# The up projection as one 512-column matmul per weight block, with both halves' sums ahead of a weight split, and that split on VectorE alone

## The reference, cut to what matters

```python
D_MODEL = 2048; SEQ = 256; GRID_W = 64; D_FF = 5632

def conv_glu_ffn(h, w_up, conv_w, w_down, grid):
    up = h @ w_up                          # (256, 2048) @ (2048, 11264)
    up = dwconv2d_grid(up, conv_w) if grid else dwconv1d(up, conv_w[1])
    a, b = jnp.split(up, 2, axis=-1)
    return (jax.nn.silu(a) * b) @ w_down   # (256, 5632) @ (5632, 2048)
```

## Time and profile before

| | before |
|---|---|
| median of three executions | 2902.12 us |
| profiled execution, its own time | 2901.94 us |
| its span | 2899.9 us |
| TensorE busy | 2783.1 us (96%) |
| VectorE busy | 1893.0 us (65%) |
| ScalarE busy | 996.5 us (34%) |
| GpSimd busy | 567.7 us (20%) |
| stretch of the 22 passes of the up projection | 2111.8 to 2626.9 us |
| in it from 2143.1: TensorE / VectorE busy | 483.8 / 433.1 of 483.8 us |

### The profile page before, as it was taken

One profiled execution on the slowest core, in us unless ns is written; L12 is line 12 of the kernel. 1 busy time (PEld: TensorE's weight loads), 2 busy tenths in 40 slices (PEclk: granted clock), 3 DMA queues, 4 the chain that ended last, 5 costly groups with the idle time before them and its releaser, 6 DMA issues.

```text
span 2899.9 us, 66324 instructions
## 1 busy us (share of the span) xinstructions
PE 2783.1 (96%) x25890; PEld 2094.7 (72%) x25890; DVE 1893.0 (65%) x3509; ACT 996.5 (34%) x1684; POOL 567.7 (20%) x708
## 2 busy tenths in 40 slices
PE   5899999999999999999988999999899999999997
PEld 1346666656666665666655888887789999998886
DVE  1136776666777666777675656564588999896444
ACT  1133333233333223333221433333344444443332
POOL 0012322223321222331220200000023333330000
PEclk8899999999999999999999999999999999999999
DMA  8721233321223322223234545554535555554554
GB/s 329 325 81 57 89 103 110 104 97 57 88 96 110 110 96 65 83 88 110 81 105 157 191 163 193 181 188 168 187 123 182 186 178 186 177 184 160 185 183 138
DMA packets 75801, 412.84 MB, mean 142 GB/s; under 512 B 9296, under 2 KB 11984, under 8 KB 42608
## 3 DMA queue, kind: packets, MB, share of 16 engines
q1 hardware_dynamic: 74864, 408.10, 40.5%
q0 software_dynamic: 768, 2.10, 0.2%
HBM read 405.38 MB, written 4.19 MB: 141 GB/s over the span
## 4 chain that ended last, share of the span: by engine, by line
PE 90%; DVE 4%; DMA 2%; ACT 2%; issue 1%; SPq 0%; DVEq 0%; ACTq 0%; PEldq 0%
PE PB L714 21%; PE Q L977 12%; PE Q L972 6%; PE PB L972 4%; PE PB L967 4%; PE CH L972 3%; PE PB L968 3%; PE CH L967 3%; PE CH L968 3%; PE Q L850 3%; PE Q L836 3%; DMA ring<-w_mod_dram 2%; PE Q L857 2%; PE CH L891 2%; PE CH L873 2%; PE CH L901 1%
## 5 line engine op out<-in xcount | busy, mean ns | idle before, releaser
L714 PE MATMUL PB<-hT,ring 128*128 128x512 f32 (+1 forms) x1536 | 670.7, 551 | 1.0
L1703 DVE TENSOR_TENSOR w_lo_r<-ring,w_hi_r 128x1536 fp32r<-128x1536 f32 (+3 forms) x178 | 389.9, 2190 | 204.4 <-ACT w_hi_r L1290 204.4
L1290 ACT ACTIVATE w_hi_r<-ring 128x2048 fp32r<-128x2048 f32 (+2 forms) x178 | 325.8, 1830 | 314.2 <-PE PB L972 104.0
L714 PEld LDWEIGHTS PB<-hT,ring 128*128 128x128 f32 x1536 | 256.1, 189 | 114.3 <-issue 69.8
L968 PE MATMUL PB<-hT_r,w_hi_r 128*128 128x256 f32 x832 | 204.7, 286 | 0.0
L1989 POOL TENSOR_TENSOR w_lo_r<-ring,w_hi_r 128x512 fp32r<-128x512 f32 x88 | 118.1, 1342 | 356.9 <-ACT w_hi_r L1290 356.9
L1878 DVE TENSOR_TENSOR w_lo_r<-ring,w_hi_r 128x1408 fp32r<-128x1408 f32 x62 | 100.7, 1626 | 131.9 <-ACT w_hi_r L1409 131.9
L1558 DVE SCALAR_TENSOR_TENSOR arena<-ring,csilp,arena 128x512 f32<-128x512 f32 x240 | 180.5, 752 | 6.1 <-DMA ring<-w_mod_dram 1.5
L967 PE MATMUL PB<-hT_r,w_hi_r 128*128 128x256 f32 x704 | 175.9, 289 | 2.8 <-DVE hT_r L1805 2.8
L977 PE MATMUL Q<-ff_r,w_hi_r 128*128 128x512 f32 x704 | 174.4, 395 | 3.5 <-ACT w_hi_r L1409 3.5
L967 PE MATMUL CH<-hT_r,w_hi_r 128*128 128x256 f32 x704 | 170.9, 283 | 0.0
(11 more groups left out here) (268 smaller groups left out, 5335.8 us busy)
## 6 DMA issues: line engine op xcount, KB each, us to landing
ring<-w_up_dram SPq DMA_DIRECT2D x88, 1024.0 KB, 4.8
ring<-w_mod_dram SPq DMA_DIRECT2D x128, 512.0 KB, 3.6
ring<-w_rkv_dram SPq DMA_DIRECT2D x48, 1024.0 KB, 6.0
ring<-w_down_dram SPq DMA_DIRECT2D x64, 704.0 KB, 4.0
ring<-w_mod_dram SPq DMA_DIRECT2D x32, 1024.0 KB, 9.3
ring<-w_ga_dram SPq DMA_DIRECT2D x16, 1024.0 KB, 4.8
ring<-w_gb_dram SPq DMA_DIRECT2D x16, 1024.0 KB, 4.9
ring<-w_pa_dram SPq DMA_DIRECT2D x16, 1024.0 KB, 4.9
```

The source lines that it names most:

```text
L714: last = mm(PB[slot % 2][:, 0:cols], tile(n, kt), hT[:, kt, 0:cols], start=(kt == 0), stop=(kt == KT - 1))
L1290: f(w_hi_r[:, r % 2, 0:n], ring[:, r, 0:n], ACT.Copy).then_inc(hi_rdy, 1)
L1703: tt(w_lo_r[:, r, 0:n], ring[:, r, 0:n], as_f32(w_hi_r[:, r % 2, 0:n]), ALU.subtract).then_inc(lo_rdy, 1)
```

## The change

Of each up tile, the first two products are now one matmul of 512 columns: 16 of them write the whole bank (`hT_r[:, kt]` holds low activations in columns 0 to 255 and high ones in 256 to 511), and the 16 of the low weight are added to the upper half of the bank. The two halves then have to be added. ScalarE copies the lower half to SBUF (`us[r]`, 256 columns, new), VectorE adds the upper half from PSUM to it (`add_halves`, new), and from then on the centre tap and all other taps read `us[r]` in SBUF. The adds of tiles 0 and 1 stand ahead of `low` of tile 2, and those of tiles 2 and 3 ahead of `low` of the next tile 0. The bank is free again after its add (`up_sum`), not after the taps. In the diff come TensorE's part, ScalarE's, VectorE's four and GpSimd's, in this order. `low` covers all 2048 columns, and GpSimd's part of it is gone; GpSimd keeps `ff_split`.

```diff
-POOL_COLS = 4 * P
+        us = [woven_sb[:, r].rearrange("p c t -> p (c t)")[:, 0:T] for r in range(4)]
...
             def up_four(i, first):
                 for r in range(4):
                     high_ready("up", i, r)
-                    pe.wait_ge(up_cv, i * 2 + 1 + r // 2)
+                    pe.wait_ge(up_sum, i * 4 + r + 1)
                     for kt in range(KT):
                         if first and r == 0:
                             pe.wait_ge(h_rdy, KT + kt + 1)
-                        with_high(four[r][:, 0:T], r, kt, h2_hi_r[:, kt], h2_lo_r[:, kt], kt == 0)
+                        mm(four[r][:, :], w_hi_r[:, r % 2, kt * P:(kt + 1) * P], hT_r[:, kt], start=(kt == 0), stop=False)
                     low_ready("up", i, r)
-                    pe.wait_ge(up_lo, i * 4 + r + 1)
                     for kt in range(KT):
-                        last = with_low(four[r][:, 0:T], r, kt, h2_hi_r[:, kt], kt == KT - 1)
+                        last = with_low(four[r][:, T:TT], r, kt, h2_hi_r[:, kt], kt == KT - 1)
...
                     if r % 2 == 0:
+                        act.wait_ge(up_cv, i * 2 + r // 2 + 1)
+                    f(us[r], four[r][:, 0:T], ACT.Copy).then_inc(up_half, 1)
+                    if r % 2:
                         act.wait_ge(ff_rdy, i * 2 + r // 2 + 1)
-                    f(cv[r], four[r][:, 0:T], ACT.Identity, scale=convw_a[:, r, 4:5]).then_inc(up_mid, 1)
+                        for q in (r - 1, r):
+                            act.wait_ge(up_sum, i * 4 + q + 5)
+                            f(cv[q], us[q], ACT.Identity, scale=convw_a[:, q, 4:5]).then_inc(up_mid, 1)
...
-                r, n = r % 4, width(phase, r % 4) - (POOL_COLS if phase == "up" else 0)
+                r, n = r % 4, width(phase, r % 4)
...
-                        last = stt(grid(cv[r])[:, orow, ocol], grid(four[r][:, 0:T])[:, irow, icol],
+                        last = stt(grid(cv[r])[:, orow, ocol], grid(us[r])[:, irow, icol],
...
+            def add_halves(i, r):
+
+                dve.wait_ge(up_half, i * 4 + r + 1)
+                tt(us[r], us[r], four[r][:, T:TT], ALU.add).then_inc(up_sum, 1)
...
                     taps(i - 1, 1, 1, carry)
+                add_halves(i, 0)
+                add_halves(i, 1)
                 lows("up", i, 0, FT // 2, "down")
...
                 taps(i, 0, 1, prev)
+                add_halves(i, 2)
+                add_halves(i, 3)
                 lows("up", i, 2, FT // 2, "down")
...
-                    pool.wait_ge(hi_rdy, split_count("up", i, r))
-                    pool.sem_inc(seen, 1)
-                    nc.gpsimd.tensor_tensor(w_lo_r[:, r, REG - POOL_COLS:], ring[:, r, REG - POOL_COLS:],
-                                            as_f32(w_hi_r[:, r % 2, REG - POOL_COLS:]), ALU.subtract).then_inc(up_lo, 1)
```

More of the change, by code:

```diff
@@ L337, in layer_kernel @@
         pool_lo = sem("activation_low_ready")
-        up_lo = sem("up_weight_low_ready")
         h2_raw = sem("h2_ready")
@@ L354, in layer_kernel @@
         xr_ld = sem("x_reloaded")
+        up_half = sem("up_low_activation_half_copied")
+        up_sum = sem("up_halves_added")
         up_mid = sem("up_centre_tap_done")
@@ L1068, in _ @@
             pe.sem_inc(up_cv, 2)
+            pe.sem_inc(up_sum, 4)
             pe.sem_inc(ff_rdy, 2)
@@ L1813, in taps @@
             def taps(i, j, half, prev):
-                if half == 0:
-                    dve.wait_ge(up_mid, i * 4 + 2 * j + 2)
                 for n in range(4 * half, 4 * half + 4):
@@ L1823, in taps @@
                         ocol, icol = slice(max(0, -b), GRID - max(0, b)), slice(max(0, b), GRID - max(0, -b))
-                        if n:
+                        if n == 0:
+                            dve.wait_ge(up_mid, i * 4 + r + 1)
+                        else:
                             V.need(prev[q])
                         w = 3 * (a + 1) + b + 1
-                        last = stt(grid(cv[r])[:, orow, ocol], grid(four[r][:, 0:T])[:, irow, icol],
+                        last = stt(grid(cv[r])[:, orow, ocol], grid(us[r])[:, irow, icol],
                                    convw_v[:, r, w:w + 1], grid(cv[r])[:, orow, ocol], ALU.mult, ALU.add)
```

## The result

The changed kernel takes 2911.18 us (median of 7 executions, 2909.42 to 2911.49), the kernel before on the same chip 2902.51 (median of 7). The ratio is 1.0025, 95% interval 1.0014 to 1.0036: 8.7 us slower by the medians. The forecast was 2910, 7.7 slower.

What follows compares the result with a forecast made beforehand. TensorE bounds the kernel before; with the change VectorE would, at 23.29 us a pass against 23.04. 2.4 + 21 x (23.29 - 23.04) = 7.7 us slower, 2910 us; its own range 2905 to 2916, widened to 2886 to 2918.

Steps and rivals of the forecast that it cites:

- TensorE's gain of 0.76 us a pass: Up projection: merged 512-column matmuls make a tile 5.57 us instead of 5.76, a pass 22.28 instead of 23.04.
- The splits cost nothing more: VectorE, up projection: four splits of 2048 columns without GpSimd's share take 8.84 us a pass, 0.1 cheaper than before.
- Taps from SBUF at the pace of those from PSUM: VectorE, up projection: eight taps still take 2.72 us, four groups 10.88 a pass, no gain or loss from SBUF.
- a sign of being wrong: The prediction is wrong if, among other signs, taps from SBUF run at another pace than from PSUM.
- Adds at 0.34: VectorE, up projection: four new adds of 256 columns take 0.34 us each, 1.36 a pass, judged by `gated`.
- The loss beside GpSimd, 1.34 us a pass: Eight taps beside `ff_split` lose 0.60 to 0.76 us, taken as 0.67, twice a pass in the up projection.
- The step that said GpSimd gets its turn at VectorE's next instruction: Where VectorE was first, GpSimd goes next; VectorE loses GpSimd's length less 0.27: cast 0.13, subtraction 0.47 us.
- The lock: Two-SBUF-input VectorE instructions and GpSimd's SBUF reads share ports exclusively; the loser blocks, by the rows less than whole length.
- the rival at 2930: Whole blocking: VectorE stands the full 1.15 us beside `ff_split`, 24.25 us a pass, 27.8 slower; chance 4%.
- The pass: Up projection: VectorE needs 21.95 + 1.34 = 23.29 us a pass, above TensorE's 22.28 and today's 23.04.
- The start, 2.4 us: First pass of the up projection: pair 1's first taps begin 2.4 us later, at 2146.2 against 2143.80.
- The end, nothing: Last half pass before the down projection: one more 0.67 us lost, about 0.68 saved on a 1408-column split.

Runs made afterwards that it cites:

- the run with the width alone: The kernel before, with only VectorE splitting all 2048 columns and GpSimd none; ratio 0.9996, 2903.58 us.
- the last kernel: Changed kernel with the halves' sum in PSUM, plus ScalarE rounding the down projection's third and fourth regions ahead of the last silu; ratio 0.9938, 2885.91 us.

## Why the prediction was right, point by point

- **TensorE's gain of 0.76 us a pass.** Right: with VectorE out of the way a pass is 22.27 us, against 22.28 forecast.
- **The splits cost nothing more.** Right, by the run with the width alone. ("About 2.3 each" before is too high: with 20.66 us busy in a pass and 11.75 for the rest, the four splits took 8.9, which is where the 0.1 us saved comes from.)
- **Taps from SBUF at the pace of those from PSUM.** Nearly: eight without GpSimd take 2322.60 - 2319.84 = 2.76 us, against 2.72; with the sum in PSUM it is 2.72 again. Four groups make 0.16 us a pass that the sum did not have. The prediction named another pace as a sign of being wrong; by the letter it came true, by 1.5%.
- **Adds at 0.34.** 0.33 measured. In the pass shown, VectorE's sum without GpSimd is 23.21 - 1.18 = 22.03 us (1.18 is worked out in the next point), with 21.95 forecast.
- **The loss beside GpSimd, 1.34 us a pass.** Right in kind, and too large: 1.18 in the pass shown, 0.61 + 0.57. For the product of pair 1, where the cast takes 0.70, it is 3.37 us for eight taps in place of 2.76: 0.61. In 11 of the 42 halves it went another way than I had it, as in the rows shown from 2313.88. There the cast gets no turn between taps and waits 2.67 us until the adds, which read only one tensor in SBUF; the taps lose nothing, and the subtraction falls beside the split, 2319.64 - 2316.87 = 2.77 in place of 2.20: 0.57. The short way costs a little more than the long one: passes take 23.27 us with it and 23.20 without. The step that said GpSimd gets its turn at VectorE's next instruction thus holds in 31 halves of 42.
- **The lock.** The page "SBUF — State Buffer" of the Trainium skill, section "SBUF: two separate sides", makes it a matter of two SBUF inputs. The rows and the run with the sum in PSUM bear that condition out exactly (3.37 against 2.72 us for eight taps). Full blocking of VectorE, the rival at 2930, was not seen: 0.57 and 0.61 us lost a half, where GpSimd's two instructions take 1.15 alone.
- **The pass.** 23.23 us in the mean, against 23.29 forecast. From the first tap of pair 1 in the first pass to the same in the last, this kernel takes 487.2 us and the one before 483.8: 3.4 more, where the sum had 5.3 less 0.7 for the narrower last split. TensorE's waits per pass are two, of 0.8 and 0.5 us in the mean at its weight loads, where I had about 1 us each.
- **The start, 2.4 us.** 3.1 measured, counted from the last instructions that make h2. The first copy of tap weights, for which I took 1.27 us from the earlier trace rows, took 0.18 here. But the low clock lasted longer: the 16 matmuls of 256 columns at the end of tile 0 took 3.62 us, where 2.08 is the length at full clock, and 2.53 before. Luck made the miss small: about 1.1 us too much for the copy stood against the lower clock, which the sum didn't have.
- **The end, nothing.** From the last pair's first tap to the third region 11.31 us against 10.58, 0.73 more where I reckoned 0.67; but the longer wait brought the low clock, 1.87 us more. That term was missing.

The four terms of the trace are 3.1 + 3.4 + 0.7 + 1.9 = 9.1 us. The spans differ by 7.7, because the profiled execution of the changed kernel was 1.4 us ahead when it reached this stage, through code that is the same in both. So the total came out well partly by luck: the passes were 1.2 us too dear in the sum (4.6 against 3.4), and that made up for most of the 1.9 that was missing at the end. The cause itself was tested from three sides: taking the second SBUF tensor away, doubling GpSimd's work, and giving its share back. Only the first tells the tensor's place from every other reason.

Open is why the cast gets its turn between taps in 31 halves and not in 11. All 11 are of pair 0, but ten passes go the short way there too, with the same instructions beside them, and with GpSimd's work doubled only one of the 42 casts took 2.67 us, the others 0.70 or 0.71. What decides it wasn't tried. That an instruction with one SBUF tensor is what ends such a wait isn't shown either: in the run with GpSimd's share kept, the share that started at 2298.87 was held off for 4.98 us and got its turn beside a tap.

## What to carry to other kernels

Before you move an operand from PSUM to SBUF, look at what GpSimd does at that time: an elementwise VectorE instruction with one tensor in each ran at full pace beside GpSimd, with both in SBUF it lost half to three quarters of GpSimd's time (0.61 of 1.15 us for taps, 0.57 of 0.74 for a split). Here the same sum, written to PSUM, turned 0.25% slower into 0.5% faster. For the same reason, a share of VectorE's work that is given to GpSimd can be worth nothing; look at the idle time of VectorE with and without it (1.27 and 1.17 us without, 1.21 and 1.17 with it), not at GpSimd's. When an engine that waited is made the bound, count its sum without the old waits, and where TensorE's longest wait grows, look at the granted clock behind it.

## What the runs showed that I had not expected

- GpSimd can be held off by a row of short VectorE instructions: a cast of 0.40 us took 2.67, in 11 of 42 places. In the run with GpSimd's share kept, a share that takes 1.29 us in the kernel before took 4.91 to 4.99 in six places, beside taps and a split.
- TensorE's granted clock fell behind a wait of 5.31 us and one of 4.61, and not behind one of 3.46. It also fell in the last kernel, behind waits of 1.41 and 0.83 us with eleven short matmuls between them, so the longest single wait does not tell it. A fall cost 1.3 to 1.9 us on eleven wide matmuls (3.93 and 4.49 us from start to start in place of 2.62).
- 20 useless matmuls in the wait kept the clock up. As the matmuls behind the wait were all there was to win, that gained 1.9 us in the profile and nothing that the times can tell.
